# In a two-block transformer kernel, half of the weight chunks of six segments get their low part on GpSimd instead of VectorE

## The reference

```python
h = rms_norm(x, norm_mix[l])
proj = h @ w_in[l]
rq, rk, rv, rg, dq, dk, dv = jnp.split(proj, split_at, axis=-1)
...
o_ret = rms_norm(retention_chunkwise(rq, rk, rv).astype(x.dtype))
...
o_diff = diff_attention_causal(dq, dk, dv, lam)
...
x = x + mix @ w_out[l]
h = rms_norm(x, norm_x[l])
...
q = (h @ xq[l]).reshape(B, S, XATTN_HEADS, XATTN_DH)
```

## Time and profile before

| what | us |
|---|---|
| median of 3 runs (lowest, highest) | 1580.56 (1580.39, 1581.3) |
| the profiled execution: time | 1579.31 |
| the profiled execution: span from first to last instruction | 1577.0 |
| TensorE busy (98% of the span) | 1541.1 |
| VectorE busy (64%) | 1007.3 |
| ScalarE busy (53%) | 833.1 |
| GpSimd busy (13%) | 208.8 |

### The profile page before, as it was taken

How to read it: one execution, slowest core, us unless ns; L and a number is a source line. 1 busy time by engine, 2 the same in 40 slices (tenths; PEclk the granted TensorE clock), 3 DMA queues, 4 the chain that set the end, 5 groups by cost and what they waited for, 6 DMA issues and landing times.

```text
span 1577.0 us, 20026 instructions
## 1 busy us (share of the span) xinstructions
PE 1541.1 (98%) x7872; PEld 1250.5 (79%) x7872; DVE 1007.3 (64%) x1681; ACT 833.1 (53%) x1459; POOL 208.8 (13%) x278
## 2 busy tenths in 40 slices
PE   9999999999999999999999999999999999999999
PEld 8877677787877888888777766888778888888887
DVE  4267977866479998999787786565765333434231
ACT  5278776554456888888753434435434333333220
POOL 1000014422234100000152101111201000000000
PEclk9999999999999999999999999999999999999999
DMA  6122121114548999999833111031212323223232
GB/s 234 63 80 81 54 80 56 54 54 158 206 161 245 382 421 421 423 421 422 290 150 107 54 54 54 28 107 54 80 54 81 99 89 107 84 90 121 67 109 92
DMA packets 78641, 235.89 MB, mean 150 GB/s; under 512 B 6960, under 2 KB 9424, under 8 KB 66256
## 3 DMA queue, kind: packets, MB, share of 16 engines
q1 hardware_dynamic: 68288, 207.62, 36.1%
q10 hardware_dynamic: 6624, 14.88, 2.5%
q0 software_dynamic: 3632, 12.08, 2.0%
HBM read 221.97 MB, written 12.60 MB: 149 GB/s over the span
## 4 chain that ended last, share of the span: by engine, by line
PE 82%; DVE 10%; ACT 3%; DMA 2%; issue 1%; POOL 1%; SPq 0%; DVEq 0%; ACTq 0%; POOLq 0%
PE bank L109 79%; PE bank L112 4%; DVE low L134 2%; DVE REST L124 1%; DVE REST L134 1%; ACT REST L115 1%; DVE REST L137 1%; DMA slot<-in_w_in 1%; ACT REST L118 1%; DVE AL L124 1%; ACT CHH L118 1%; DVE REST L146 1%; DVE REST L143 1%; DVE REST L130 1%; DVE st L140 0%
## 5 line engine op out<-in xcount | busy, mean ns | idle before, releaser
L124 DVE TENSOR_TENSOR low<-slot,CHH 128x1024 fp32r<-128x1024 f32 (+1 forms) x300 | 297.7, 1035 | 116.9 <-ACT CHH L118 115.9
L118 ACT ACTIVATE CHH<-slot 128x1024 fp32r<-128x1024 f32 (+1 forms) x300 | 259.0, 901 | 128.0 <-PE bank L109 56.6
L134 DVE SCALAR_TENSOR_TENSOR low<-slot,smalls,CHH 128x512 fp32r<-128x512 f32 (+1 forms) x232 | 170.3, 765 | 192.9 <-ACT CHH L118 192.7
L109 PE MATMUL bank<-AH,CHH 128*128 128x512 f32 (+1 forms) x640 | 248.5, 388 | 0.2 <-DVE AL L124 0.2
L109 PE MATMUL bank<-AL,CHH 128*128 128x512 f32 (+1 forms) x640 | 242.9, 379 | 0.0
L109 PE MATMUL bank<-AH,low 128*128 128x512 f32 (+1 forms) x640 | 242.6, 379 | 0.0
L118 ACT ACTIVATE CHH<-slot,smalls 128x512 fp32r<-128x512 f32 (+1 forms) x232 | 154.7, 701 | 138.3 <-PE bank L109 68.6
L109 PE MATMUL bank<-CHH,AH 128*128 128x512 f32 x512 | 216.3, 422 | 5.3 <-ACT REST L118 3.8
L109 PE MATMUL bank<-low,AH 128*128 128x512 f32 x512 | 201.7, 394 | 0.0
L109 PE MATMUL bank<-CHH,AL 128*128 128x512 f32 x512 | 201.2, 393 | 0.0
L109 PE MATMUL bank<-CHH,XTF 128*128 128x512 f32 x512 | 161.3, 396 | 1.9 <-DVE REST L121 1.0
(11 more groups left out here) (189 smaller groups left out, 2391.0 us busy)
## 6 DMA issues: line engine op xcount, KB each, us to landing
slot<-in_w_in SPq DMA_DIRECT2D x35, 1024.0 KB, 5.1
slot<-in_w_exp_gate SPq DMA_DIRECT2D x32, 1024.0 KB, 13.6
slot<-in_w_exp_up SPq DMA_DIRECT2D x32, 1024.0 KB, 13.5
slot<-in_w_exp_down SPq DMA_DIRECT2D x32, 1024.0 KB, 14.0
slot<-in_w_gate SPq DMA_DIRECT2D x10, 1024.0 KB, 5.0
slot<-in_w_up SPq DMA_DIRECT2D x10, 1024.0 KB, 4.9
slot<-in_w_down SPq DMA_DIRECT2D x10, 1024.0 KB, 5.0
slot<-in_w_out SPq DMA_DIRECT2D x8, 1024.0 KB, 5.7
```

What stands on the lines that cost most here:

```text
L109: return self.e.matmul(out, l, r, start=start, stop=stop) if self.e else Issued()
L118: return self.e.activation(out, in_, ACT.Copy, scale=scale) if self.e else Issued()
L124: return self.e.tensor_tensor(out, a, b, op) if self.e else Issued()
L134: return self.e.scalar_tensor_tensor(out=out, in0=a, scalar=s, in1=b, op0=op0, op1=op1) if self.e else Issued()
```

## The change

`by_pool` holds the odd chunks (k = 1, 3, 5, 7) of the six segments, 24 of 48. For these, ScalarE first multiplies the raw chunk by its gain in place, waits for the end of that, and writes the high part by a copy without a scale. VectorE passes over the chunk. GpSimd subtracts the high part from the scaled chunk, a TENSOR_TENSOR of two operands in SBUF, and signals on a semaphore of its own, `pool_lo`. On GpSimd `split_chunks` is called at the same steps as on the two others, and its `seg` for dv, rq, rk, rv now counts by rows too.

```diff
+    by_pool = {c for name in ("dv", "rq", "rk", "rv", "xq0", "xq1") for c in range(SEG[name][0], SEG[name][0] + KT) if c % 2}
...
-                    x = act.copy(high(c), raw(c), scale=gain_at[c])
+                    if c in by_pool:
+                        own(act.copy(raw(c), raw(c), scale=gain_at[c]))
+                        x = act.copy(high(c), raw(c))
+                    else:
+                        x = act.copy(high(c), raw(c), scale=gain_at[c])
...
                 c = next_chunk[0]
+                next_chunk[0] += 1
+                if c in by_pool:
+                    continue
                 dve.wait_ge(*at(("", "hi", c)))
...
+        lows = sorted(by_pool)
+
+        def split_chunks(upto):
+
+            while lows and lows[0] <= upto:
+                c = lows.pop(0)
+                pool.wait_ge(*at(("", "hi", c)))
+                pool.tt(low(c), raw(c), high(c).bitcast(F32), ALU.subtract).then_inc(*mark("pool_lo", ("", "lo", c)))
+
         def seg(name, evac=None, rows=False):
-            nk = SEG[name][1]
+            c0, nk, nj, _ = SEG[name]
             for k, j in steps_of(name, rows):
+                if rows and j == nj - 1:
+                    split_chunks(c0 + k + 5)
+                elif rows and j == 0:
+                    split_chunks(min(c0 + k + 5, c0 + 7))
                 if evac and k == nk - 1:
                     evac(j)
                 yield
...
-        interleave(pool.stepping(chain(*(seg(x) for x in ("dv", "rq", "rk", "rv")))), df_gen)
+        interleave(pool.stepping(chain(*(seg(x, rows=True) for x in ("dv", "rq", "rk", "rv")))), df_gen)
```

More of the change, by code:

```diff
@@ L2128, in split_chunks @@
                 x.then_inc(*mark("dve_lo", ("", "lo", c)))
-                next_chunk[0] += 1
         def ahead(c, far):
```

## The result

| | before | after |
|---|---|---|
| median of 6 runs each on one chip (lowest to highest), us | 1579.64 (1575.33 to 1581.3) | 1586.76 (1586.34 to 1587.6) |
| profiled execution: time, span, us | 1579.31, 1577.0 | 1586.39, 1584.5 |

The ratio is 1.0051 with a 95% interval of 1.0038 to 1.0063: the change makes the kernel slower by 0.5%, 8 us by the ratio (6 to 10), where +5.5 was forecast.

The account below looks back on a forecast made before the run. TensorE, busy 1541.1 of 1577.0 us, was taken to bound the kernel. Six segment terms summed to 6.0 us, less about 0.5 returned, +5.5; from a median of 1580.56 this gave 1586.0 us, range 1581.0 to 1591.0.

Parts of the forecast that it names:

- rk: Segment rk's burst: added copies and GpSimd's subtractions delay low 4, the rotary group and TensorE's link; +1.7 us (0.7 to 2.6).
- dv: Segment dv's burst: low 6 and the maximum behind it wait, so TensorE's exponentials come later; +1.0 us (0.2 to 1.3).
- The 0.5 us that later waits were to return: Small later waits in the stretch, found shorter by a delayed TensorE, return about 0.5 us of the 6.0 sum.
- the port: Shared SBUF port: during a GpSimd subtraction, VectorE's instructions with two SBUF operands stand; one case took 2.96 us more.
- one more us: In rk, GpSimd's chunk 7 can hold a two-operand tensor-tensor and TensorE's link one us more, up to +2.6.
- rq: Segment rq's burst: chunk 7 late (0.6) and the reciprocal root behind it in GpSimd's queue (0.6); +1.2 us (0.3 to 1.9).
- rv: Segment rv's burst: a ScalarE copy 0.8 later, VectorE's relief mostly taken back by the port; +0.5 us (-0.8 to 1.5).
- xq0: Segment xq0, no attention beside it: plain stall of TensorE for GpSimd's chunk 7, ready at 1088.4; +1.0 us (0.8 to 1.3).
- xq1: Segment xq1: GpSimd's chunk 5 holds low 6 and links behind it, on which TensorE's wait hangs; +0.6 us (0.1 to 1.2).
- VectorE's relief wins: Rival: waits behind bursts of lows shrink, 3.9 us come back, 1576.6 us; chance 7%.
- Absorbed: Rival: only xq0's plain stall and about half a us elsewhere remain, 1582 us; chance 24%.
- The port and GpSimd's queue dominate: Rival: each of 24 subtractions holds VectorE 1.3 us and queued roots come late; +10, 1591 us; chance 14%.

Follow-up runs that it names:

- The last pair of experiments: VectorE's lows of dv, rq, rk and rv one step later, in the kernel before (1577.67 us, ratio 0.9999) and in the changed kernel (1581.24 us, 1.0025).
- e2_subtract: Changed kernel without the scaled copy in place: GpSimd subtracts for the 24 odd chunks, ScalarE copies as before; 1578.08 us, ratio 1.000 to the kernel before.
- e3_relief: Kernel before, but nobody makes the odd chunks' low parts; TensorE takes the high part twice; 1572.18 us, ratio 0.9964.
- e5_dummy_set: Kernel before, plus three memsets on GpSimd whenever an odd chunk's high part is ready, 24 times; VectorE keeps all lows; 1577.92 us, ratio 0.9999.
- e1_copies: Changed kernel with only ScalarE's added copies; VectorE makes all low parts, GpSimd none; 1582.44 us, ratio 1.0032 to the kernel before.
- e7_early: The change for chunks 1 and 3 of each of the six segments only; 1581.6 us, ratio 1.0026 to the kernel before.
- e8_late: The change for chunks 5 and 7 of each of the six segments only; 1582.37 us, ratio 1.0029 to the kernel before.

## Why the prediction was right, and where it wasn't

The sign and the size class held, and four of six terms lie in their ranges; rk and dv lie above theirs. 1586.0 was forecast and 1586.76 measured, but so close a hit is luck in part: the forecast stood on a median of 1580.56 for the kernel before, which is 1579.64 over six runs, so the change costs 7.1 us by the medians (8 by the ratio) where 5.5 was forecast. The 0.5 us that later waits were to return did not come: the sum of 8.0 is still there at 1150 us. Two readings of the forecast were loose without bearing on a term: a low takes 0.71 us of queue by the earlier trace rows (28.4 over 40), not 0.67, and among the rows of the port there is no operation that reads PSUM, so that these aren't held was first shown by the masks above. Terms against the table:

**rk, +1.7 forecast, +2.99 measured: the mis-sized term.** The chain was the one worked out. Timeline of the kernel after: ScalarE, VectorE, GpSimd, TensorE, against the earlier trace rows:

```profile
923.64 0.71 ACT L118 ACTIVATE CHH<-slot,st 128x512 fp32r<-128x512 f32 x1
...
924.38 1.27 DVE L134 SCALAR_TENSOR_TENSOR low<-slot,st,CHH 128x512 fp32r<-128x512 f32 x1 [1.14 <-ACT CHH L118]
925.57 1.65 DVE L134 SCALAR_TENSOR_TENSOR REST<-bank,st,consts 128x256 f32<-128x256 f32 x4
...
928.12 1.21 DVE L124 TENSOR_TENSOR st<-st 128x1 f32<-128x1 f32 x1
...
929.68 0.35 DVE L134 SCALAR_TENSOR_TENSOR REST<-REST,st 128x128 f32<-128x128 f32 x1
...
923.81 1.29 POOL L124 TENSOR_TENSOR low<-slot,CHH 128x512 fp32r<-128x512 f32 x1 [1.30 <-ACT CHH L118]
...
928.05 1.26 POOL L124 TENSOR_TENSOR low<-slot,CHH 128x512 fp32r<-128x512 f32 x1
...
930.09 0.33 PE L112 MATMUL bank<-consts,REST 128*128 128x128 f32 x1 [3.73 <-DVE REST L134]
```

Low 4 waits 1.14 us for ScalarE and takes 1.27 beside GpSimd's chunk 3, since that began 0.57 earlier. The rotary group starts at 925.57; taking off the 3.75 us that TensorE was late already, that is 921.82 instead of 920.44, +1.38, inside the 1.05 to 1.65 forecast. Then a tensor-tensor of one element per partition stands for 1.21 us instead of 0.16 from just after the start of GpSimd's chunk 7 to its end: the "one more us", in full. The link ends 2.42 us later; I had taken 2.1. Later waits return 0.9 where I had given back 0.4, so the chain itself comes to about +1.5, close to the +1.7 forecast. What I missed is behind the link: a stretch at half clock adds 1.5 (931.6 to 935.0 us). It is tied to the wait, though not by a fixed rule: in six traces TensorE waits 2.2 to 3.7 us for this link and the stretch follows in five, in the other six it waits 0.6 to 1.7 us and no stretch follows. The last pair of experiments shows that the place of the lows is the lever: with low 4 behind the rotary group (and all other lows of the four segments a step later too), rk is +0.33.

**dv, +1.0 forecast, +1.53.** The path is right, the cause I gave only half of it. VectorE's last low of the burst holds the maximum and so the exponentials, as forecast. But I had the port in front of that low, and the copies alone give +1.20; relief and subtractions together take off 0.36 (`e2_subtract`). The stall for GpSimd's chunks lies ahead of the exponentials' wait and shortens it, as I had put it. VectorE and TensorE after:

```profile
859.69 1.25 DVE L134 SCALAR_TENSOR_TENSOR low<-slot,st,CHH 128x512 fp32r<-128x512 f32 x1 [1.99 <-ACT CHH L118]
...
860.44 0.50 PE L109 MATMUL bank<-CHH,AH 128*128 128x512 f32 x1 [1.27 <-POOL low L124]
862.35 0.50 PE L109 MATMUL bank<-CHH,AH 128*128 128x512 f32 x1 [0.27 <-POOL low L124]
864.00 1.04 PE L109 MATMUL bank<-REST 64*128 64x256 f32 x4 [0.69 <-ACT REST L115]
```

The three waits sum to 2.2 us where one of 1.23 was the earlier trace rows.

**rq, +1.2 forecast, +1.20: right in size, and in mechanism in part.** I had 0.6 for chunk 7 and 0.6 for the root behind it in GpSimd's queue. What TensorE waits for first is a link that I had not named, which GpSimd's chunk 7 holds by the port. Kernel after:

```profile
893.55 0.75 DVE L134 SCALAR_TENSOR_TENSOR low<-slot,st,CHH 128x512 fp32r<-128x512 f32 x1 [1.23 <-ACT CHH L118]
...
894.93 1.38 DVE L134 SCALAR_TENSOR_TENSOR REST<-REST,st 128x128 f32<-128x128 f32 x1
...
894.88 1.29 POOL L124 TENSOR_TENSOR low<-slot,CHH 128x512 fp32r<-128x512 f32 x1 [2.83 <-ACT CHH L118]
...
897.11 0.35 DVE L130 TENSOR_SCALAR REST<-bank,st 128x128 f32<-128x128 f32 x1 [0.79 <-POOL st L124]
...
896.37 0.33 PE L112 MATMUL bank<-consts,REST 128*128 128x128 f32 x1 [0.43 <-DVE REST L134]
...
897.51 0.33 PE L112 MATMUL bank<-consts,REST 128*128 128x128 f32 x1
```

The held link ends at 896.31 and adds 0.60 to TensorE. GpSimd's low of chunk 7, which the next step needs, ends at 896.17, and TensorE would have come to it at 895.80 (893.03 in the trace of before, 2.77 us late by now): without the held link it would have waited for the chunk almost as long. Then the root counts after all. VectorE's scaling waits 0.79 us for it and ends at 897.46, and TensorE's transpose of the scaled rows starts right behind, at 897.51: another 0.33.

In the run with late chunks alone the same link is held for 1.38 us and the root is late too, but less:

```profile
889.16 0.75 DVE L134 SCALAR_TENSOR_TENSOR low<-slot,st,CHH 128x512 fp32r<-128x512 f32 x1 [1.24 <-ACT CHH L118]
...
890.53 1.38 DVE L134 SCALAR_TENSOR_TENSOR REST<-REST,st 128x128 f32<-128x128 f32 x1
...
892.13 0.55 POOL L124 TENSOR_TENSOR st<-st 128x1 f32<-128x1 f32 x1
...
892.45 0.27 PE L112 MATMUL bank<-consts,REST 128*128 128x128 f32 x1
```

Its root ends at 892.68, 1.4 us later than before by TensorE's time (891.80 less 0.55), and TensorE loses 0.02: so much lateness of the root costs nothing yet (in the kernel after it is 2.5 us). The link ends at 891.91, inside the slack of 0.9 that it had. Only with the early chunks' copies in front too, which put it another 1.07 later (VectorE's low 6 at 893.55 less 2.77 against 889.16 plus 0.55), does it come too late. So rq is what the two halves do together: +0.11 and +0.02 apart, +1.20 in one. The two waits make up 0.9 of the 1.20; the rest isn't settled.

**rv, +0.5 forecast, +0.54.** Right net. It is a relief of 1.93 (`e3_relief`) taken back by the subtractions (+2.9 between that kernel and `e2_subtract`); "the port takes most of it back" was too mild, it takes all and 0.9 more. The wait of 1.54 is 1.82 at 973.68 now.

**xq0 and xq1, +1.0 and +0.6 forecast, +0.99 and +0.79.** The plain stall is there, and in xq1 a wait of 0.23 for a low of GpSimd and the one for a link, 1.34 instead of 1.06; timeline of TensorE after:

```profile
1095.57 0.50 PE L109 MATMUL bank<-CHH,AH 128*128 128x512 f32 x1 [0.65 <-POOL low L124]
...
1124.00 0.44 PE L112 MATMUL bank<-consts,REST 128*128 128x128 f32 x2 [1.34 <-DVE REST L130]
```

In xq1 the copies alone already give +1.1. In xq0 they give +0.4 (0.3 in the burst itself): the rest of its stall is GpSimd's 1.3 us. For xq0 my sum holds a slip that came out well: from 1085.5 the two added copies less the gaps lead to 1086.5, and I wrote 1087.1. In the kernel after, taking off TensorE's 7.3 us, the high part is ready at 1086.8 and the low at 1088.2 (forecast: 1088.4), so the term stands nearer to what I wrote than to my own terms.

**The rivals.** "VectorE's relief wins" fell, but its mechanism is worth 6 us, not 3.9; it failed since GpSimd's subtractions cost as much again, and the copies 4 to 5 more. "Absorbed" fell: nothing of the six terms came back later. "The port and GpSimd's queue dominate" is nearer than I gave it (14%): about half of the cost before relief is the subtractions. The parts, by the table: relief -4.7, subtractions +7.2, copies +4.3, together +6.9 of 8.0. The 1.1 left is what they do only together, of which rq holds 0.8. Without the stretches at half clock it is -4.7, +5.8 and +2.8, +3.9 of 6.5: then 2.6 us arise only together. How the subtractions' part divides between the port and the queue in the changed kernel isn't measured by itself. For the port speak the memsets, which sit in the same queue for longer and cost nothing, and that TensorE never waits for a low of GpSimd in `e2_subtract`.

**The signs** named ahead: subtractions of 1.26 to 1.44 us (said 1.3 to 1.9), lows over 0.85 us (0.91, 0.94), two-operand instructions of 1.5 us and more (the longest 1.8), waits of 11.0 (said about 11), a wait for a GpSimd low in xq0 (0.65, said about 1), the wait near 923.92 grown, no wait over 2 us for a chunk (1.27). One is missing: TensorE's waits for lows in 850 to 1000 us are both dv's, none is at rq's chunk 7.

## What to carry to other kernels

Moving an operation off the busiest helper engine buys what its queue loses in front of late links, but ask what the new engine's instruction does to the old one: here the relief (6 us) and what the subtractions cost (6 us by the medians) cancel, and the copies that the move adds on a third engine decide. Where one instruction with its gain becomes two on two engines, both queues pay. A copy in ScalarE's spare time isn't free when a low part and then a link stand behind it, even at 43% load. And where an instruction stands in a burst matters more once something ahead of it is late: the same move by one step was worth nothing before the change and 2.6 us after it. And when parts are measured one by one, see whether each trace has the same stretches at half clock, or the sum can come out right by accident.

## What the runs showed of the hardware that I had not expected

**One SBUF operand can be held too.** In the kernel after, a TENSOR_SCALAR from SBUF to SBUF with one tensor operand took 1.39 us beside a GpSimd subtraction that had begun 0.05 earlier, where the same form takes 0.35:

```profile
1115.10 1.39 DVE L130 TENSOR_SCALAR REST<-REST,st 128x256 f32<-128x256 f32 x1
...
1115.05 1.30 POOL L124 TENSOR_TENSOR low<-slot,CHH 128x512 fp32r<-128x512 f32 x1 [0.61 <-ACT CHH L118]
```

Beside memsets, which read nothing, this form is held as well. In `e5_dummy_set` three memsets run from 889.59 to 891.29, and a TENSOR_SCALAR that takes 0.29 elsewhere took 0.69:

```profile
890.67 0.69 DVE L130 TENSOR_SCALAR REST<-REST,st 128x128 f32<-128x128 f32 x1
...
889.59 1.70 POOL L149 MEMSET seg<- 128x512 f32 x3 [1.56 <-ACT CHH L118]
```

So memsets are not free for VectorE in general: all told they lengthened its TENSOR_SCALARs between 850 and 1132 us by 1.8 us, at places that cost this kernel nothing. My prediction counted operations with two SBUF operands only. The Trainium skill has this rule ("SBUF — State Buffer", section "SBUF: two separate sides"): `tensor_scalar` can run in a mode that uses both port pairs and contends then. These rows agree with it.

**Half-clock stretches come and go.** Windows (start:end, length, engines, PEclk, DMA share, GB/s) of the kernel after, then of the kernel before, then of the kernel after where the same instructions of TensorE run:

```profile
931.00:935.00 4.00, 4.00 (x16) 3.33 (x15) 3.40 (x11) 1.29 (x6) 0.78 (x2) 0.57 0.00 0
```

```profile
1153.00:1156.40 3.40, 3.40 (x10) 2.71 (x9) 1.07 (x2) 1.57 (x4) 0.00 (x0) 0.53 0.00 0
```

```profile
1160.00:1164.00 4.00, 2.87 (x14) 2.43 (x14) 1.61 (x5) 1.20 (x4) 0.49 (x1) 1.00 0.00 0
```

A granted clock of 0.57 and 0.53 over such windows is close to the lower level, 1.2 of 2.4 GHz, for most of them. In the first, TensorE had waited 3.73 us and worked 1.5 us since. In before, it had waited 1.85 us at 1152.05; in after it waits 1.84 at the same instruction (1161.13), and the clock stays at 1.00. The stretch in before costs 1.6 us, which the profiled execution of after is spared. Of the twelve kernels profiled, four have it and eight don't, though all waited 1.84 or 1.85 us there. Others of 1 to 3 us come and go near 448 and 803 us, where no kernel here differs from another: they make up the +1.0 us that after has ahead of all changed chunks, and in the other kernels between -3.0 and +0.9. So the profiled spans differ by some us for this reason alone, and for a term of 1 us the difference by segment says more than the span. By the granted clocks on record, these stretches are also what spreads the runs of one kernel over 5 us (1575.33 to 1581.3 before). Over the 77 runs of the kernel before that the experiments brought, on three chips, the span falls by 1.0 to 1.2 us for each 0.001 of granted clock (correlation -0.83 to -0.92 by chip), and in `e1_copies` the fastest run, 1578.56 us, had 0.999 and the slowest, 1589.21, had 0.992. By such lines, at equal granted clock, `e7_early` is +1.3 us in span and `e8_late` +3.3 (estimates, which leave out what the stretches cost), where the changed kernel is +6.7 to +8.0: again the halves don't add up to the whole.
